# The byte at which a kernel's tensors start: expert weights at multiples of 128, turned activations 64 bytes off the weights

## The reference

```python
# first block: latent attention and retention, cross attention, then a mixture of 32 experts
h = rms_norm(x, attn_norm_g);  proj = h @ w_in
x = x + concat(a_out, r_out) @ w_out
x = x + memory_cross_attention(hc, m, ...)
a = einsum('sd,edf->sef', hr, w_gate)      # 32 experts, 1024 x 256 each
u = einsum('sd,edf->sef', hr, w_up)
x = x + einsum('sef,efd->sd', silu(a) * u * gate, w_down)
# second block: recurrence and convolution, 7 groups of columns from w_in, gated FFN, a last gate
z = rmsnorm(x, g_mix) @ w_in_2             # 1024 x 7168
rnn_x = causal_depthwise_conv(rnn_x, conv4_w) + conv4_b; y_rnn = gelu(rnn_y) * rg_lru(rnn_x, ...)
x = x + merged @ w_out_2
g, u = split(h @ w_gate_up, 2);  x = x + (silu(g) * u) @ w_down
x = x + sigmoid(rmsnorm(x, g_ple) @ w_ple_gate) * (p_i @ w_ple)
```

## The kernel before, in words

| tensors | past a multiple of 128 |
|---|---|
| stage, w_hi, w_lo, whole, x, xs, xT, aT, cT, y_hi, y_lo, turned_unit, rows_unit, hT, rx_hi, rx_lo, over_queries, over_turned, xg | 0 |
| hidden_unit, hidden, silu_t, silu_g, token_now, hiddenT, embed, arena, over_values, over_scores, raw_turned, over_latent, slot_of | 64 |
| spent_unit, spent, norm_g | 32 |

## Time and profile before

### The profile page before, as it was taken

One profiled execution on the slowest core, in us unless ns is written; L12 is line 12 of the kernel. 1 busy time (PEld: TensorE's weight loads), 2 busy tenths in 40 slices (PEclk: granted clock), 3 DMA queues, 4 the chain that ended last, 5 costly groups with the idle time before them and its releaser, 6 DMA issues.

```text
span 856.8 us, 13811 instructions
## 1 busy us (share of the span) xinstructions
PE 809.6 (94%) x5562; PEld 667.3 (78%) x5562; DVE 496.4 (58%) x835; ACT 416.3 (49%) x708; POOL 20.1 (2%) x41
## 2 busy tenths in 40 slices
PE   9999999999999877597979999999999999999996
PEld 7888888888865544244459999999988888888885
DVE  6667777856531210111168988888876555555486
ACT  5777488665411100000266757575746444444365
POOL 1600000000000000000000000000000000000000
PEclk9999999999999987899999999999999999999999
DMA  9855522978899999999975555555574665655421
GB/s 325 267 188 184 181 102 99 371 266 314 319 416 420 420 420 421 421 421 420 407 267 179 194 189 179 183 183 176 192 245 148 226 191 196 196 173 188 178 99 50
DMA packets 95184, 214.47 MB, mean 250 GB/s; under 512 B 4728, under 2 KB 59552, under 8 KB 81824
## 3 DMA queue, kind: packets, MB, share of 16 engines
q1 hardware_dynamic: 93456, 211.70, 67.8%
q0 software_dynamic: 1376, 1.89, 0.8%
q10 hardware_dynamic: 304, 0.20, 0.1%
HBM read 212.72 MB, written 1.05 MB: 249 GB/s over the span
## 4 chain that ended last, share of the span: by engine, by line
PE 79%; SPq 13%; DMA 4%; DVE 2%; ACT 1%; issue 1%; DVEq 0%; ACTq 0%
SPq L831 13%; PE bank L2244 13%; PE bank L2246 13%; PE bank L2245 13%; PE bank L3034 6%; PE bank L3035 6%; PE bank L3033 6%; PE bank L2261 4%; DMA over_queries<-in_expert_w_up_dram 3%; PE bank L2257 3%; PE bank L2754 3%; PE bank L2251 2%; PE bank L2252 2%; PE bank L2742 1%; PE bank L2787 1%; PE bank L2589 1%
## 5 line engine op out<-in xcount | busy, mean ns | idle before, releaser
L2244 PE MATMUL bank<-w_hi,xT_hi 128*128 128x512 f32 (+2 forms) x390 | 150.8, 387 | 0.0
L2246 PE MATMUL bank<-w_hi,xT_lo 128*128 128x512 f32 (+2 forms) x390 | 148.4, 381 | 0.0
L2245 PE MATMUL bank<-w_lo,xT_hi 128*128 128x512 f32 (+2 forms) x390 | 148.2, 380 | 0.0
L3033 PE MATMUL bank<-hT_hi,w_hi 128*128 128x256 f32 x440 | 124.6, 283 | 0.0
L3034 PE MATMUL bank<-hT_lo,w_hi 128*128 128x256 f32 x440 | 124.5, 283 | 0.0
L3035 PE MATMUL bank<-hT_hi,w_lo 128*128 128x256 f32 x440 | 124.5, 283 | 0.0
L452 DVE TENSOR_TENSOR w_lo<-stage,w_hi 128x1024 fp32r<-128x1024 f32 (+3 forms) x78 | 87.8, 1126 | 31.7 <-ACT w_hi L438 30.8
L438 ACT ACTIVATE w_hi<-stage 128x1024 fp32r<-128x1024 f32 (+3 forms) x80 | 78.6, 983 | 27.7 <-PE bank L2246 13.3
L454 DVE TENSOR_TENSOR w_lo<-stage,w_hi 128x1024 fp32r<-128x1024 f32 (+3 forms) x78 | 87.5, 1122 | 0.0
L3034 PEld LDWEIGHTS bank<-hT_lo,w_hi 128*128 128x128 f32 x440 | 84.5, 192 | 0.0
L3035 PEld LDWEIGHTS bank<-hT_hi,w_lo 128*128 128x128 f32 x440 | 84.5, 192 | 0.0
(11 more groups left out here) (505 smaller groups left out, 1660.8 us busy)
## 6 DMA issues: line engine op xcount, KB each, us to landing
stage<-in_w_in_dram SPq DMA_DIRECT2D x36, 1024.0 KB, 5.1
stage<-in_w_gate_up_dram SPq DMA_DIRECT2D x44, 512.0 KB, 4.7
stage<-in_w_down_dram SPq DMA_DIRECT2D x11, 1024.0 KB, 4.8
whole<-in_expert_w_up_dram SPq DMA_DIRECT2D x10, 1024.0 KB, 25.4
stage<-in_w_out_dram SPq DMA_DIRECT2D x8, 1024.0 KB, 5.1
whole<-in_expert_w_gate_dram SPq DMA_DIRECT2D x8, 1024.0 KB, 23.4
stage<-in_cross_w_kv_dram SPq DMA_DIRECT2D x7, 1024.0 KB, 8.8
stage<-in_expert_w_gate_dram SPq DMA_DIRECT2D x7, 1024.0 KB, 13.0
```

What stands on the lines that cost most here:

```text
L2244: mm(o, k_hi, v_hi, start=start, stop=False)
L2245: mm(o, k_hi, v_lo, start=False, stop=False)
L2246: return mm(o, k_lo, v_hi, start=False, stop=stop)
L3033: mm(o, w_hi[:, s, at:at + P], hT_hi[:, k, :], start=k == 0, stop=False)
```

## The change

Fillers of 64, 128, 96 and 96 bytes are put before xT, after turned_unit, after const and before hidden. hot_rank and left_gates get no tensor of their own any more, but lie in biased and exps. token_gates moves, and the filler unused2 shrinks.

```diff
-    turned_memory, (xT_hi, xT_lo, aT_hi, aT_lo, cT_hi, cT_lo) = parts(
-        ("xT_hi", [P, KD, 2 * P], F32R), ("xT_lo", [P, KD, 2 * P], F32R), ("aT_hi", [P, 2, 2 * P], F32R),
+    turned_memory, (_, xT_hi, xT_lo, aT_hi, aT_lo, cT_hi, cT_lo) = parts(
+        ("turned_apart", [P, 16], F32), ("xT_hi", [P, KD, 2 * P], F32R), ("xT_lo", [P, KD, 2 * P], F32R), ("aT_hi", [P, 2, 2 * P], F32R),
         ("aT_lo", [P, 2, 2 * P], F32R), ("cT_hi", [P, 3, 2 * P], F32R), ("cT_lo", [P, 3, 2 * P], F32R))
...
     turned_unit = sb("turned_unit", [P, SLOT])
+    sb("turned_end", [P, 32])
...
     const = sb("const", [P, KEPT_COLS])
+    sb("spent_apart", [P, 24])
...
     over_n, over_i = sb("over_n", [P, 2]), sb("over_i", [P, 2], I32)
+    sb("hidden_apart", [P, 24])
...
-    hot_rank = eb("hot_rank", [P, T, EXPERTS])
+    hot_rank, left_gates = biased[:, :, 0:EXPERTS], exps[:, :, 0:EXPERTS]
...
-    left_gates = eb("left_gates", [P, T, EXPERTS])
     x_sums, gate_scale = eb("x_sums", [P, T, 2]), eb("gate_scale", [P, T])
-    eb("unused2", [P, 74])
+    token_gates = eb("token_gates", [P, T, EXPERTS, 2])
+    eb("unused2", [P, 58])
...
-            nc.vector.tensor_copy(hot_rank[:], ranks)
+            nc.vector.tensor_copy(hot_rank, ranks)
...
-            stt(left_gates[:], hot_rank[:], OWN + STRIP - 0.5, token_gates[:, :, :, 0], ALU.is_gt, ALU.mult)
+            stt(left_gates, hot_rank, OWN + STRIP - 0.5, token_gates[:, :, :, 0], ALU.is_gt, ALU.mult)
```

More of the change, by code:

```diff
@@ L289, in program @@
     route = xg[:].rearrange("p k s -> p (k s)")[:, 0:9 * T * EXPERTS].rearrange("p (a n) -> p a n", a=9)
-    token_gates = eb("token_gates", [P, T, EXPERTS, 2])
     expert_memory.close()
```

## The result

| | before | after |
|---|---|---|
| median of 5 runs each | 860.44 us (858.68 to 861.84) | 865.08 us (863.38 to 865.72) |
| ratio after to before | | 1.0055, 95% interval 1.0038 to 1.0072 |
| profiled execution, its span | 858.64 us, 856.8 us | 865.43 us, 863.6 us |
| mean granted TensorE clock | 0.980 | 0.975 |

The forecast was 855.4 us and a chance of 0.5 for "faster". The sign is wrong. The time lies inside the range (840 to 867 us), but only because that was drawn wide enough for most of rival 3.

The account below looks back on a forecast made before the run. The pace of float32r matmuls (some 670 us) and the transfer rate (some 180 us) were taken as the bounds. Terms 0 + 0 - 6.0 + 0 took the median from 861.44 to 855.4 us, range 840 to 867.

Parts of the forecast that it names:

- rival 3: Wide products no longer settle and stay at 231 ns instead of 227: +7.3 us, 868.7 without heads' gain; chance 0.20.
- Places of the expert units: Expert stage: units moved to multiples of 128 bytes change neither TensorE's pace nor the transfer rate; 0 us.
- hot_rank and left_gates: Their new shared places cost DVE only nanoseconds, beside expert transfers lasting until 423 us; 0 us.
- Heads: 256-column products with hT or rx moving at 64: 4 ns less on each of 1512 matmuls, -6.0 us.
- Wide products: 512-column products, stationary operand at 64, w moving at 0: settled pace stays at 227 ns; 0 us.
- the 240 ns of the earlier trace: Expert-stage burst of wide matmuls, stationary at 64: 240 ns each beside 230 in the like place; read as no gain.
- Rival 1: Nothing happens: the 13.3 ns are the cost of changing the stationary operand, not of addresses; 861.4 us, chance 0.30.
- the 13.3 ns a matmul: Part of every float32r matmul's pace beyond one column per cycle, whatever its width; all the change could win.
- Rival 2: Both kinds fall: 64 bytes part colliding reads, half of 13.3 ns gone from 3,200 matmuls, 21 us; 840 us, chance 0.20.

Follow-up runs that it names:

- N = 192: The changed kernel with xT, aT, cT, hT and rx 192 instead of 64 bytes on from where they are level with w; 852.4 us, one execution.
- N = 128: The changed kernel with xT, aT, cT, hT and rx 128 instead of 64 bytes on from where they are level with w; 864.4 us, one execution.

## Why the prediction was wrong

**Places of the expert units, 0.** Right. With these and the shared tiles alone the ratio is 0.9998, and the interval ends at 1.0010, 0.9 us. The 1.4 us that the prediction estimated from the 256-byte rule of the Trainium skill ("DMA: Bandwidth & Descriptors", "How a descriptor splits into AXI transactions") lie outside it; the measurement decides. The units named for the earlier trace rows were one off: by their issues and times to landing (321.62 and 26.4, 323.80 and 26.7, 325.98 and 27.8 us) turned_unit, spent_unit and embed land at 348.0, 350.5 and 353.8, so embed came in the next window, with 424 GB/s. The reading stands.

**hot_rank and left_gates, 0.** Right, by the same run.

**Heads, -6.0 us.** Right in kind, too large: -2.2 ns a matmul and not -4, so -3.1 us for 1,416, and -3.5 measured alone. The step that failed is the price, "take the 4 ns by which the load is shorter". A load's duration is no measure of the pace: it is 188 ns in the heads at 117.8 and in those at 113.3, and 188 beside wide matmuls at 227 and at 233. The gaps of the earlier trace rows, 107 to 113 ns, did not show it either (see below); the settled pace was 117.8.

**Wide products, 0.** This is the step that gave the wrong sign: "I read no gain in it and take the settled 227 as it is: 0". They went from 227.2 to 233.3, 6.1 x 1,620 = 9.9 us, and alone cost 8.9. The prediction had only one row of that kind, at 240 ns beside 230 in the like place, and used it to deny a gain.

**The rows that both steps rest on.** The earlier trace rows could not answer the question, for two reasons. First, the table of starts went by 128, and that hid the side of the difference. From the shapes, token_now begins 45,760 bytes behind y_hi, which is 192 modulo 256 and not 64. So these bursts stand for N = 192 in the sweep, where the heads have 113.5 and the wide products 229.1, and not for the 64 of the change. Second, a burst of four shows neither. In the kernel after, token_now and y are level, and its bursts take the same: 0.47 us for the wide pair that took 0.48, and 0.55 us for the four that took 0.53.

```profile
351.57 0.63 PE L2808 MATMUL bank<-y_lo,token_now 128*128 128x512 f32 x2
352.04 0.63 PE L2805 MATMUL bank<-y_hi,token_now 128*128 128x512 f32 x2
```

```profile
437.63 0.71 PE L2826 MATMUL bank<-token_now,y_hi 128*128 128x256 f32 x4 [0.84 <-ACT y_hi L1366]
438.18 0.63 PE L2833 MATMUL bank<-y_hi,token_now 128*128 128x512 f32 x2
```

That the heads' sign came out right is therefore luck in part, and the 240 ns of the earlier trace rows was no sign of the loss that came.

**The sum.** -3.1 for the heads, 9.9 for the wide products, -0.6 for the 96 narrow ones (6.1 ns each): +6.2 us beside 6.8 in the spans and 4.6 in the medians.

**The rivals.** Rival 3 is what happened, with 0.20. Its mechanism was off: the wide products do settle, but at another value, above the 231 ns that I took as the worst. So its bound for the loss, 4 ns, was too low, and the gain in the heads that was to cancel it was half as large. Rival 1 is out: the 13.3 ns a matmul are not as a whole a fixed cost of changing the stationary operand, since the same instructions at the same places in the order take 120.0 or 113.3 ns by the place of hT alone. (For the other 6.7 ns of the heads, and for the 13.3 of wide products with level operands, a fixed cost is not ruled out.) The rule of the Trainium skill beside it ("TensorE: Matmul & The Clock Gate", Part 2, step 1) does not account for this; the runs show a dependence on both operands' addresses and not by what path. Rival 2 needed both kinds to fall. At 64 only the narrow ones do, and no offset that was run brings the wide ones under 227.

**What stays open.** It is open what in the chip makes the difference modulo 256 count and what decides at the entry of a stretch between 113.3 and 117.8, or 228.9 and 233.3.

## What to carry to other kernels

In a kernel bound by float32r matmuls, treat the byte difference between the moving and the stationary operand, modulo 256, as a setting of its own for each kind of product (width, and which operand moves), and measure it: here it cost up to 12 us in 860 and gained 6.4 (median of six; 10 in its best single execution), and the best value for one kind is bad for another. Move one kind at a time; the change moved two and saw only the difference of their effects. Write starts modulo 256, with the side: 64 ahead and 64 behind are different places. Judge by the settled gap between starts in a long stretch, not by durations, loads or bursts.

## What the runs showed of the hardware that was not expected

- A float32r matmul has a settled pace for each difference, which nearly always repeats from stretch to stretch. At 256 columns it lies between 113.3 and 120.0 ns, at 512 between 226.7 and 234.3. At some places it is the mean of a repeating pattern of gaps: in the heads at N = 128, 120, 119, 115, 118 and 121 ns, over and over. None is under 106.7 or 213.3, one column per cycle at 2.4 GHz.
- It depends on how far the moving operand's start lies ahead of the stationary one's, modulo 256 bytes, in steps down to the 32 bytes that were tried. All moved by 64 gives 227.3 and 120.0 again.
- With the same program and addresses a stretch of 54 matmuls ran at 117.7 ns in one execution and 113.6 in another, and stayed at its pace to its end.
